# Router weights stationary in four column groups, memory rows and router rows transposed before they are scaled, and blocks of the start and of the routing moved

## What is computed

```python
def mem_kv(mem, g_mem_norm, w_mem_kv):
    kv = rmsnorm(mem, g_mem_norm) @ w_mem_kv          # 256 memory rows
...
    z = rmsnorm(x, g_attn_norm) @ w_in
    # windowed attention with sinks | short gated conv | attention over the memory rows
    mix = group_norm_concat([attn, conv_out, cross], g_mix_out)
    h = x + mix @ w_out
    hn = rmsnorm(h, g_ffn_norm).reshape(B * T, D_MODEL)
    y = h + moe(hn, ...)
...
def moe(x, w_router, b_router, ...):                   # 32 experts, 4 for each row
    logits = (x @ w_router) + b_router
    top_v, top_e = lax.top_k(logits, TOP_K)
    gates = jax.nn.softmax(top_v, axis=-1)
    # each expert: gate and up products, clamped SwiGLU, down product, times the gate
```

## Time and profile before

| | us |
|---|---|
| median of 3 runs | 1468.87 (1468.76 to 1469.4) |
| the profiled execution | 1467.07 |
| its span | 1465.3 |
| PE busy | 1413.5 (96%) |
| DVE busy | 1201.0 (82%) |
| ACT busy | 988.2 (67%) |
| POOL busy | 293.4 (20%) |

### The profile page before, as it was taken

One profiled execution on the slowest core, in us unless ns is written; L12 is line 12 of the kernel. 1 busy time (PEld: TensorE's weight loads), 2 busy tenths in 40 slices (PEclk: granted clock), 3 DMA queues, 4 the chain that ended last, 5 costly groups with the idle time before them and its releaser, 6 DMA issues.

```text
span 1465.3 us, 18790 instructions
## 1 busy us (share of the span) xinstructions
PE 1413.5 (96%) x6719; PEld 1028.5 (70%) x6719; DVE 1201.0 (82%) x1118; ACT 988.2 (67%) x946; POOL 293.4 (20%) x191
## 2 busy tenths in 40 slices
PE   5999999699999999999999999999999999999994
PEld 3777755477777777777777777777777777777773
DVE  2435344689999999999999999999999999999995
ACT  2134331487777777777777777777777777777773
...
GB/s 371 223 63 65 33 125 236 145 326 370 373 380 373 365 363 363 368 369 366 365 367 364 359 356 367 354 375 368 358 366 361 368 356 367 370 364 361 363 283 137
DMA packets 51575, 461.76 MB, mean 315 GB/s; under 512 B 10708, under 2 KB 14758, under 8 KB 25812
## 3 DMA queue, kind: packets, MB, share of 16 engines
...
...
## 4 chain that ended last, share of the span: by engine, by line
PE 93%; DVE 2%; issue 1%; ACT 1%; DMA 1%; POOL 0%; POOLq 0%; SPq 0%; ACTq 0%; DVEq 0%
PE psum L2051 24%; PE psum L2053 24%; PE psum L2052 24%; PE psum L1682 7%; PE psum L1842 4%; PE psum L2064 2%; PE psum L2037 2%; PE psum L2046 2%; PE psum L1654 1%; DMA area<-in_x_prompt 1%; PE psum L2027 1%; PE psum L1753 0%; PE psum L1777 0%; DVE ring L1568 0%; DMA area<-hn_tbl,idx_i 0%
## 5 line engine op out<-in xcount | busy, mean ns | idle before, releaser
L1530 DVE TENSOR_TENSOR low<-raw,high 128x2048 fp32r<-128x2048 f32 x384 | 869.7, 2286 | 36.7 <-ACT high L951 34.4
L951 ACT CAST high<-raw 128x2048 fp32r<-128x2048 f32 x384 | 724.6, 1912 | 101.1 <-PE psum L2053 101.0
L2051 PE MATMUL psum<-high,area_r 128*104 128x512 f32 x1536 | 613.3, 399 | 1.2 <-DVE area_r L1524 1.2
L2053 PE MATMUL psum<-low,area_r 128*104 128x512 f32 x1536 | 604.2, 393 | 0.0
L2052 PE MATMUL psum<-high,area_r 128*104 128x512 f32 x1536 | 603.1, 393 | 0.0
L2053 PEld LDWEIGHTS psum<-low,area_r 128*104 128x104 f32 x1536 | 258.1, 168 | 98.2
L2051 PEld LDWEIGHTS psum<-high,area_r 128*104 128x104 f32 x1536 | 258.4, 168 | 90.1 <-DVE area_r L1524 1.7
L2052 PEld LDWEIGHTS psum<-high,area_r 128*104 128x104 f32 x1536 | 258.7, 168 | 89.2
L631 POOL DMA_INDIRECT area<-hn_tbl,idx_i x33 | 94.5, 2864 | 292.3 <-DVE idx_i L1453 285.6
L615 POOL CAST pick_r<-area 64x104 fp32r (+1 forms) x33 | 31.0, 938 | 526.4 <-PE psum L2053 526.3
L1682 PE MATMUL psum<-ring 128*128 128x272 f32 x448 | 106.4, 394 | 1.2 <-DVE area L1142 0.9
...
## 6 DMA issues: line engine op xcount, KB each, us to landing
raw<-in_w_gate_up SPq DMA_DIRECT2D x128, 2048.0 KB, 10.6
raw<-in_w_down SPq DMA_DIRECT2D x64, 2048.0 KB, 10.0
ring<-in_w_in SPq DMA_DIRECT2D x7, 1024.0 KB, 20.1
...
ring<-in_w_mem_kv SPq DMA_DIRECT2D x1, 2048.0 KB, 11.3
...
ring<-in_mem_kT SPq DMA_DIRECT2D x1, 2048.0 KB, 8.3
ring<-in_cache_mem_v SPq DMA_DIRECT2D x1, 2048.0 KB, 8.2
```

Of the source, the lines that this page charges most:

```text
L951: nc.scalar.copy(high_w(i), raw_w(t)).then_inc(sem("w_high"), 1)
L1530: v.tensor_tensor(low_w(t), raw_w(t), high_w(i), ALU.subtract).then_inc(sem("w_low"), 1)
L2051: mm(bank, high, wh, start=start, stop=False)
L2053: return mm(bank, high, wl, start=False, stop=stop)
```

## The change

- Memory rows are no longer scaled before their transposition. The scale is put on by ACT where it copies the keys and values out of PSUM (`mem_out`). Loads of memory rows and of `wm` are split in two, and `mem_kv` runs in four half blocks.
- Router: `router_rows(j)` transposes the unscaled h (`hrow`), the FFN gain is multiplied into `wr` once, and the row scale comes in `logits`. `router(j)` holds the router weights stationary, 32 columns in each of four column groups, which work on four contraction tiles side by side; ACT copies the four partial sums out (`logits_T`), and `router_sums(j)` adds and transposes them by one product with `eye2`.
- Blocks moved: small set-up work and `gain` on DVE, bias copies on ACT, `mq_diagonals` behind both `denominators` of unit 1, the gates and places of tiles 0 to 2 before the last tiles, the slot number of expert 0 by a product of its own ahead of the gates, one `low_part` before the flag and one after the first `x_low`.

The diff, cut to its core:

```diff
@@ -324,10 +325,10 @@
-                                                                          ("lg", _j - 1, 0), ("part", _j, 4), ("part", _j, 5)]
-        RING += [("ss", NTT - 1, 0), ("group", NTT - 1, 0), ("group", NTT - 1, 1), ("sum", NTT - 1, 0), ("sum", NTT - 1, 1)]
-        for _j in (NTT - 2, NTT - 1):
-            RING += [("hT", _j, 0), ("hT", _j, 1), ("lg", _j, 0)]
+                                                                          ("hT", _j - 1, 2), ("part", _j, 4), ("lg", _j - 1, 0), ("part", _j, 5)]
+        RING += [("ss", NTT - 1, 0), ("group", NTT - 1, 0), ("group", NTT - 1, 1), ("hT", NTT - 2, 0), ("hT", NTT - 2, 1),
+                 ("sum", NTT - 1, 0), ("sum", NTT - 1, 1), ("hT", NTT - 2, 2), ("lg", NTT - 2, 0), ("hT", NTT - 1, 0), ("hT", NTT - 1, 1),
+                 ("hT", NTT - 1, 2), ("lg", NTT - 1, 0)]
@@ -389,8 +390,11 @@
-            sp.dma_start(memrow, mem_prompt[0].rearrange("(m p) d -> p m d", p=P)).then_inc(sem("ld_mem"), 16)
-            sp.dma_start(wm, w_mem_kv[0].rearrange("(k p) n -> p k n", p=P)).then_inc(sem("ld_wm"), 16)
+            for m in range(2):
+                sp.dma_start(memrow[:, m, :], mem_prompt[0, m * P:(m + 1) * P, :]).then_inc(sem(f"ld_mem{m}"), 16)
+            for half in range(2):
+                ks = slice(half * 4, half * 4 + 4)
+                sp.dma_start(wm[:, ks, :], w_mem_kv[0].rearrange("(k p) n -> p k n", p=P)[:, ks, :]).then_inc(sem(f"ld_wm{half}"), 16)
@@ -728,27 +732,29 @@
-                if r == 0:
-                    ac.wait_ge(sem("ld_mem"), 16)
-                elif r >= 2:
-                    ac.wait_ge(sem(f"ld_x{r - 2}"), 16)
+                ac.wait_ge(sem(f"ld_mem{r}" if r < 2 else f"ld_x{r - 2}"), 16)
...
+            def mem_out(m):
+                ac.wait_ge(sem("rs_ready"), m + 1)
+                ac.wait_ge(sem("mkv_pe"), m + 1)
+                nc.scalar.activation(mkv[:, m, :], banks[4 + m][:, :], ACT.Copy, scale=rs7[:, m:m + 1]).then_inc(sem("mkv_ready"), 1)
...
+            mem_out(0)
...
+            mem_out(1)
+            ac.wait_ge(sem("mkv_pe"), 3)
+            nc.scalar.copy(view(ring, 7424, [512]), banks[4][:, :]).then_inc(sem("mkT_ready"), 1)
...
-            for m in range(2):
-                ac.wait_ge(sem("mkv_pe"), m + 1)
-                nc.scalar.copy(mkv[:, m, :], banks[4 + m][:, :]).then_inc(sem("mkv_ready"), 1)
-            ac.wait_ge(sem("mkT_pe"), 1)
-            nc.scalar.copy(view(ring, 7424, [512]), banks[7][:, :]).then_inc(sem("mkT_ready"), 1)
@@ -834,9 +840,14 @@
-                    ac.wait_ge(sem("hT_pe"), 2 * j + half + 1)
+                    ac.wait_ge(sem("hT_pe"), 3 * j + half + 1)
...
+            def logits_T(j):
+                n = ROWS[j]
+                ac.wait_ge(sem("hT_pe"), 3 * j + 3)
+                nc.scalar.copy(lgT[:, j % 2, 0:n], ring_bank("hT", j, 2)[:, 0:n]).then_inc(sem("hT_ready"), 1)
@@ -1113,27 +1128,16 @@
-            for r in range(9):
+            for r in range(2):
+                ms(r)
+                rows_T(r)
+            for r in range(2, 9):
...
-                if 1 <= r < 8:
+                if 3 <= r < 8:
...
-                if r >= 2:
+                if r >= 4:
@@ -1276,10 +1280,13 @@
+            def h_mean(j):
+                n = ROWS[j]
+                dv.wait_ge(sem("ssh_raw"), j + 1)
+                v.tensor_scalar(ssh[0:n, j:j + 1], ssh[0:n, j:j + 1], 1.0 / D, EPS, ALU.mult, ALU.add).then_inc(sem("ssh_ready"), 1)
...
-                dv.wait_ge(sem("ssh_raw"), j + 1)
-                v.tensor_scalar(ssh[0:n, j:j + 1], ssh[0:n, j:j + 1], 1.0 / D, EPS, ALU.mult, ALU.add).then_inc(sem("ssh_ready"), 1)
@@ -1287,9 +1294,10 @@
-                v.tensor_tensor(lg[0:n, j, 0:NE], ring_bank("lg", j, 0)[0:n, 0:NE], brt[0:n, :], ALU.add).then_inc(sem("lg_ready"), 1)
+                v.scalar_tensor_tensor(out=lg[0:n, j, 0:NE], in0=ring_bank("lg", j, 0)[0:n, 0:NE], scalar=rsh[0:n, j:j + 1], in1=brt[0:n, :],
+                                       op0=ALU.mult, op1=ALU.add).then_inc(sem("lg_ready"), 1)
@@ -1334,22 +1342,31 @@
-            z_even(8)
-            z_even(0)
+            for t in (8, 0, 1, 2, 3):
+                z_even(t)
+            dv.wait_ge(sem("ld_sm"), 48)
+            link(v.tensor_tensor(selt, sink[:, 0:8], c_("sel"), ALU.mult))
+            v.tensor_tensor(wr, wr, vec(G_FFN, KD).broadcast_to([P, KD, NE]), ALU.mult).then_inc(sem("wo_ready"), 1)
+            link(v.reduce_sum(sink[:, 8:9], selt, axis=AX.X))
+            link(v.tensor_copy(sink[:, 9:10], sink[:, 8:9]))
+            link(v.tensor_scalar(sink8, sink, 1.0 / SCALE, None, ALU.mult))
...
+            scores(0)
+            gain(0)
+            gain(1)
+            z_even(13)
...
-            z_even(1)
-            for t in range(4):
-                gain(t)
-            z_even(2)
-            for t in range(4, 8):
-                gain(t)
-            z_even(3)
-            scores(0)
-            z_even(13)
@@ -1361,17 +1378,22 @@
             z_even(7)
-            mq_diagonals()
+            for t in range(2, 5):
+                gain(t)
...
             denominators(1, 1)
+            mq_diagonals()
             scores(2)
             z_even(9)
+            gain(5)
...
             z_even(11)
+            gain(6)
+            gain(7)
@@ -1424,19 +1447,24 @@
+                    gates(0, NTT - 2, P, 1)
+                h_mean(j)
...
+            places(0, NTT - 2, P)
+            first_slots(0, NTT - 2)
...
+            h_mean(NTT - 1)
...
-            gates(0, NTT - 1, P, 1)
-            places(0, NTT - 1, P)
-            first_slots(0, NTT - 1)
...
-            gates(NTT - 1, NTT, NSM, 2)
-            places(NTT - 1, NTT, NSM)
-            first_slots(NTT - 1, NTT).then_inc(sem("hot_ready"), 1)
+            places(NTT - 2, NTT, P)
+            first_slots(NTT - 2, NTT).then_inc(sem("hot_ready"), 1)
+            gates(NTT - 2, NTT - 1, P, 2)
+            dv.wait_ge(sem("pos_pe"), NTT + 1)
+            v.tensor_scalar(idx_i[0:CAP, 0:1], banks[6][0:CAP, 416:417], float(NT), None, ALU.add).then_inc(sem("idx_ready"), 1)
+            gates(NTT - 1, NTT, NSM, 3)
@@ -1445,19 +1473,27 @@
-                v.tensor_reduce(gcol[0:CAP, k % UB:k % UB + 1], info[:, 1:3], AX.X, ALU.add).then_inc(sem("gcol_ready"), 1)
...
+                v.tensor_reduce(gcol[0:CAP, k % UB:k % UB + 1], info[:, 2:4], AX.X, ALU.add).then_inc(sem("gcol_ready"), 1)
...
+            def low_part(n, i, last=False):
...
+                t = half_at(i, last)[1]
+                dv.wait_ge(sem("w_high"), place(n, i) + 1)
+                v.tensor_tensor(low_w(t), raw_w(t), high_w(i), ALU.subtract).then_inc(sem("w_low"), 1)
...
+            low_part(-1, 10, True)
...
+            slot_info(0, 0, again=False)
@@ -1551,6 +1581,8 @@
+                if not m:
+                    low_part(m - 1, 11, True)
@@ -1649,34 +1681,36 @@
-            def mem_kv(m):
-                for k in range(KD):
+            def mem_kv(m, half):
+                pe.wait_ge(sem(f"ld_wm{half}"), 16)
+                for k in range(half * 4, half * 4 + 4):
...
-                last.then_inc(sem("mkv_pe"), 1)
+                if half == 1:
+                    last.then_inc(sem("mkv_pe"), 1)
...
-            pe.wait_ge(sem("ld_wm"), 16)
+            pe.wait_ge(sem("xT_ready"), 2)
+            mem_kv(0, 0)
...
-            mem_kv(0)
+            mem_kv(1, 0)
+            mem_kv(0, 1)
...
-            mem_kv(1)
+            mem_kv(1, 1)
...
+            pe.wait_ge(sem("mkv_ready"), 2)
...
-                pe.wait_ge(sem("mkv_ready"), m + 1)
...
-                    last = tr(banks[7][:, c * 256 + m * P:c * 256 + (m + 1) * P], mkv[:, m, c * P:(c + 1) * P], ident)
-            last.then_inc(sem("mkT_pe"), 1)
+                    last = tr(banks[4][:, c * 256 + m * P:c * 256 + (m + 1) * P], mkv[:, m, c * P:(c + 1) * P], ident)
+            last.then_inc(sem("mkv_pe"), 1)
...
-                if i == 0 and half == 1:
-                    pe.wait_ge(sem("mkT_ready"), 1)
@@ -1877,21 +1912,29 @@
-                pe.wait_ge(sem("hn_ready"), j + 1)
+                pe.wait_ge(sem("h_part"), 6 * (j + 1) if j < NTT - 1 else 6 * j + 2)
...
-                        last = tr(bank[:, k * P:k * P + n], hnr[0:n, par, kk * P:(kk + 1) * P], ident[0:n, 0:n])
+                        last = tr(bank[:, k * P:k * P + n], hrow[0:n, par, kk * P:(kk + 1) * P], ident[0:n, 0:n])
...
-                pe.wait_ge(sem("hT_ready"), 2 * j + 2)
+                pe.wait_ge(sem("hT_ready"), 3 * j + 2)
+                bank = ring("hT", j, 2)
+                for t in range(2):
+                    for g in range(4):
+                        last = mm(bank[g * NE:(g + 1) * NE, 0:n], wr[:, 4 * t + g, :], hnT[:, par, 4 * t + g, 0:n], start=(t == 0), stop=(t == 1))
+                last.then_inc(sem("hT_pe"), 1)
...
+            def router_sums(j):
...
+                n = ROWS[j]
+                pe.wait_ge(sem("hT_ready"), 3 * j + 3)
...
-                for k in range(KD):
```

(16 more changed lines are left out.)

95 lines of the change are left out of this document (47 added, 48 removed).

## The result

The changed kernel takes 1449.52 us in the median of four runs (1448.12 to 1450.99), the kernel before 1469.13 us beside it (1468.76 to 1469.63, four runs). The ratio is 0.9866, with a 95% interval from 0.9849 to 0.9883: some 19.6 us less. The profiled execution of the changed kernel took 1450.99 us, the longest of its four, with a span of 1449.2 us.

The account below looks back on a forecast made before the run. PE was taken as the bound in its busy stretches, with the chains of waits at the start and the routing's end. 9.5 + 0.9 + 2.3 + 2.8 + 2.9 = 18.4 us off 1467.07, plus 1.8, gave 1450.5 us; range 1446.5 to 1458.

Parts of the forecast that it names:

- Start: Memory products before z: first product at 9.8 us instead of 19.13, z at 31.1 us, 9.5 us earlier.
- the slow records: First mem_kv records: run at half pace, 1.2 GHz rather than 2.4; some 1.3 us added for three of them.
- Bias stall: PE's wait among the z blocks for bank 6, behind DVE's bias subtractions: gone, 0.9 us, at worst 0.
- Stall in unit 1: PE's wait at 111.74 us for mq_diagonals, denominators and POOL: POOL now runs before PE asks, 2.3 us gained.
- what is late next: scores(2) on DVE, behind the diagonals, only 0.2 us earlier; PE needs its result some 5 us after it is ready.
- Router: Routers of tiles 0 to 2: 0.78 us each with the sum product instead of 1.71, 2.8 us gained in all.
- groups that don't pay: Rival at the router: drains or serial work turn 2.8 us into -0.6, giving 1454 to 1455 us; chance 0.07.
- End of the routing: Last tile's sums to expert 0's first rows: rows at 280.9 us against 283.85, 2.9 us gained.
- no slack: ACT's weight copies before expert 0: rows transposed 9.52 us after they begin, no slack between; so 280.5 us.
- DVE's flag: Before expert 0: ends at about 279.1 us behind a low_part of 2.3 us; PE loads it by 280.7 us.
- the landing by the rule: First gather beside DVE's low_part: shared port delays it up to 2.3 us, to 281.3 us, costing 0.4 us.
- a longer expert: Expert loop: an expert period longer than before would show the prediction wrong.

Follow-up runs that it names:

- changed_again: The changed kernel with no edit, run once more; 1450.03 us, ratio 0.9876 to the kernel before.
- orders_undone: The changed kernel with the bias copies and subtractions and the memory diagonals back in their old places; 1462.62 us, ratio 0.9961.
- mq_late: The changed kernel with DVE building the memory diagonals behind the scores of unit 2 instead of ahead; 1448.90 us, ratio 0.9870.
- router_one_group: The changed kernel with all eight router products in one column group of 32 and a sum product over 32 rows; 1457.43 us, ratio 0.9925.
- low_late: The changed kernel with DVE's first low_part for the first expert behind the flag instead of ahead of it; 1448.50 us, ratio 0.9868.
- start_undone: The changed kernel with memory loads whole, memory rows scaled before transposition and DVE's first loop staggered as before; 1459.05 us, ratio 0.9938.

## Why the prediction was right, step by step

The time was forecast at 1450.5 us and is 1449.52. The parts, from the profiled execution of after against that of before:

- **Start**, 9.5 us forecast: 8.98 in that trace, 11.0 in changed_again. The traces of before and after both have four slow records, so 8.98 compares like with like, and changed_again has none. The first product (9.8 forecast, 9.94) and the working to z hold. The prediction calls the slow records half pace by the clock; their doubled time is in the rows, but the granted clock reads 1.00 beside them. What it did not see is that this term rests on the next one: without the new order of the bias copies the biases, which in orders_undone are there only at 53.8 us, would have held it back.
- **Bias stall**, 0.9 us: from z to the first scores 38.54 us before and 37.41 after, 1.1 us. As a saving against the trace of before it is right; as the price of the old order after this start it is 9.75 us, 7.96 of them a wait.
- **Stall in unit 1**, 2.3 us: 1.6. The step that failed is "what is late next": the 5 us of cover given to `scores(2)` were not there, and POOL came 0.77 us late one unit on. mq_late shows the cause.
- **Router**, 2.8 us: 0.79 a tile, 2.4. The router (0.58, forecast 0.57) is as priced and the sum product (0.14, forecast 0.21) cheaper. But the four records of `part` behind each take 0.08 and 0.06 us more than in a long run, and the four ahead of the router 0.07 (203.78 to 205.59 us). The Trainium skill, TensorEngine Tiling (Array Packing), Tiling Modes, has the engine drained at a change of mode. After's rows put the way out of the router's mode at 0.08 us, and since its sum product changes no mode and costs nearly the same behind it, they don't show that this is a drain. router_one_group, whose sum product has a mode of its own (32*128), speaks for one: the four records ahead of it take 1.91 us instead of 1.82, and it takes 0.34 instead of 0.14 itself, 0.29 us for two changes of mode. That it works on 32 rows instead of 128 differs too, so the drain stays unproven. The rival, groups that don't pay, fell with router_one_group.
- **End of the routing**, 2.9 us: 16.43 - 14.05 = 2.38 (14.05 us are the offset of the last tile's `part`, 257.69 and 243.64 us). ACT began at 257.10 us, as forecast (271.0 - 14.05 = 256.95). But its chain has 0.9 us more room than the prediction, which said "no slack", read off before, where the gather ended last too (1.33 us of waiting for it): in low_late the rows follow ACT's first cast by 8.62 us, not 9.52. Nor did DVE's flag hold the head: it ends at 263.2 us, 277.2 in the prediction's times, not 279.1. So the gather decides, which the prediction had as its exception and not in its sum, and the landing by the rule, 281.3 - 14.05 = 267.25 us, is the nearest figure to the 267.42 measured. By the Trainium skill, SBUF — State Buffer, on the two separate sides, the loser of the shared port waits for the whole instruction: 1.29 + 2.27 would be 3.56 us, and 3.53 are measured. The same section gives the port to whoever starts first, and that these rows don't show: the gather's row starts 0.09 us ahead and still waits, and where it runs free with DVE's operation 0.18 us behind it (start_undone, router_one_group), that operation takes its 2.27 us all the same.

These make 16.4 us. Not in the sum were 1.2 us gained between the first rows and expert 1, where the full clock came back sooner, and 1.6 us lost in the expert loop: 16.1 us in the span. The medians differ by 3.5 us more than that, because the profiled execution of before was 2.1 us faster than its median and that of after 1.5 us slower. So the forecast of 1450.5 us is nearer than its sum, and by luck: the sum is 2.3 us too large for the profiled pair, and after's median lies 1.5 us below its profiled execution, not 1.8 us above it; the two errors cancel but for 1.0 us. (The upper bounds of the terms add up to 21.4 us, not 21.6; the range doesn't hang on it.) It had also named a longer expert as a sign that it would be wrong: the sign came, at 0.05 us, too small to turn the result.
